# Hybrid DeltaNet, MoBA and RG-LRU block: norm weights and identity packed with the input into two transfers, first roundings and lows dealt in pairs, z's products waiting for each operand apart

## The reference, cut to what matters

```python
def rms_norm(x, w):
    xf = x.astype(jnp.float32)
    y = xf * lax.rsqrt(jnp.mean(xf * xf, axis=-1, keepdims=True) + NORM_EPS)
    return (y * w.astype(jnp.float32)).astype(x.dtype)

for l in range(DEPTH):
    h = rms_norm(x, norm_mix[l])
    proj = h @ w_in[l]
    (dq, dk, dv, dz, da, db, mq, mk, mv, lx, ly, gates) = split_columns(proj)
    y_dn = gated_deltanet(dq, dk, dv, dz, ...) @ dn_out[l]
    y_mb = moba_attention(mq, mk, mv) @ mb_out[l]
    y_lru = rg_lru_branch(lx, ly, ...) @ lru_out[l]
    ...
    x = x + mixed @ w_o[l]
    h = rms_norm(x, norm_ffn[l])
    gate, up = jnp.split(h @ ffn_in[l], 2, axis=-1)
    x = x + (jax.nn.silu(gate) * up) @ ffn_down[l]
return rms_norm(x, norm_final)
```

## Time and profile before

| | us |
|---|---|
| median of 3 runs | 909.99 |
| lowest and highest of them | 909.69, 910.98 |
| profiled execution: span, first to last instruction | 907.7 |
| TensorE busy in it | 895.2 |
| VectorE busy | 664.6 |
| ScalarE busy | 510.9 |

### The profile page before, as it was taken

How to read it: one execution, slowest core, us unless ns; L and a number is a source line. 1 busy time by engine, 2 the same in 40 slices (tenths; PEclk the granted TensorE clock), 3 DMA queues, 4 the chain that set the end, 5 groups by cost and what they waited for, 6 DMA issues and landing times.

```text
span 907.7 us, 13854 instructions
## 1 busy us (share of the span) xinstructions
PE 895.2 (99%) x5436; PEld 763.3 (84%) x5436; DVE 664.6 (73%) x1102; ACT 510.9 (56%) x871; POOL 2.4 (0%) x6
## 2 busy tenths in 40 slices
PE   8999999999999999999999999999999999999996
PEld 5999898888888888888779998988888888888885
DVE  6879877778958665756688798767988675665656
ACT  7586555685446444445475866558744554444443
POOL 0000000000000000000000000000000000000000
PEclk9999999999999999999999999999999999999999
DMA  8645436657665667677655343386567467768761
GB/s 308 196 159 163 145 113 160 232 201 241 211 209 159 216 210 247 201 226 250 204 166 182 123 164 124 109 233 231 195 205 241 149 216 217 246 191 259 223 203 47
DMA packets 111985, 176.37 MB, mean 194 GB/s; under 512 B 65584, under 2 KB 71472, under 8 KB 111920
## 3 DMA queue, kind: packets, MB, share of 16 engines
q1 hardware_dynamic: 111632, 175.40, 60.3%
q10 hardware_dynamic: 288, 0.08, 0.0%
HBM read 167.06 MB, written 8.39 MB: 193 GB/s over the span
## 4 chain that ended last, share of the span: by engine, by line
PE 91%; DVE 4%; ACT 2%; DMA 1%; issue 1%; SPq 0%; ACTq 0%; DVEq 0%
PE bank L456 7%; PE bank L455 7%; PE bank L454 7%; PE bank L552 7%; PE bank L554 7%; PE bank L553 7%; PE bank L357 5%; PE bank L358 5%; PE bank L359 5%; PE bank L629 5%; PE bank L396 5%; PE bank L397 5%; PE bank L398 5%; PE bank L386 2%; PE bank L384 2%; PE bank L385 2%
## 5 line engine op out<-in xcount | busy, mean ns | idle before, releaser
L882 ACT CAST whi<-raw 128x1024 fp32r<-128x1024 f32 x292 | 305.8, 1053 | 295.1 <-PE bank L456 90.0
L1218 DVE TENSOR_TENSOR wlo<-raw,whi 128x1024 fp32r<-128x1024 f32 x292 | 349.8, 1217 | 63.4 <-ACT whi L882 60.6
L357 PE MATMUL bank<-ahi,whi 128*128 128x256 f32 x448 | 129.6, 289 | 0.8 <-DVE tmp L1268 0.8
L358 PE MATMUL bank<-alo,whi 128*128 128x256 f32 x448 | 126.6, 283 | 0.0
L359 PE MATMUL bank<-ahi,wlo 128*128 128x256 f32 x448 | 126.6, 283 | 0.0
L552 PE MATMUL bank<-whi,ahi 128*128 128x512 f32 x288 | 114.8, 399 | 1.5 <-DVE alo L1282 0.8
L554 PE MATMUL bank<-whi,alo 128*128 128x512 f32 x288 | 112.3, 390 | 0.0
L553 PE MATMUL bank<-wlo,ahi 128*128 128x512 f32 x288 | 112.2, 390 | 0.0
L454 PE MATMUL bank<-whi,ahi 128*128 128x512 f32 x288 | 112.2, 390 | 0.0
L456 PE MATMUL bank<-whi,alo 128*128 128x512 f32 x288 | 112.1, 389 | 0.0
L455 PE MATMUL bank<-wlo,ahi 128*128 128x512 f32 x288 | 112.0, 389 | 0.0
(11 more groups left out here) (268 smaller groups left out, 1297.0 us busy)
## 6 DMA issues: line engine op xcount, KB each, us to landing
raw<-stream_dram SPq DMA_DIRECT2D x292, 512.0 KB, 4.6
turned_dram<-proj SPq DMA_DIRECT2D x144, 32.0 KB, 1.8
proj<-turned_dram SPq DMA_DIRECT2D x18, 256.0 KB, 4.8
proj<-gbias_dram SPq DMA_DIRECT2D x12, 256.0 KB, 4.4
probs_dram<-proj SPq DMA_DIRECT2D x8, 192.0 KB, 4.0
proj<-probs_dram SPq DMA_DIRECT2D x2, 768.0 KB, 5.9
par<-params_dram SPq DMA_DIRECT2D x2, 556.5 KB, 8.1
x<-x_dram SPq DMA_DIRECT2D x2, 512.0 KB, 5.2
```

The source lines that it names most:

```text
L357: pe.matmul(dst, whi_of(m)[:, wcol], hi, start=first, stop=False, skip_group_check=True)
L358: pe.matmul(dst, whi_of(m)[:, wcol], lo, start=False, stop=False, skip_group_check=True)
L882: act.copy(whi_of(m), raw_of(m)).then_inc(*AC.up(("hi", m), "w"))
L1218: dv.tensor_tensor(wlo_of(m), raw_of(m), whi_of(m), ALU.subtract).then_inc(*DV.up(("lo", m), "w"))
```

## The change

The norm weights (32 columns), the identity (128) and x (2 x 1024) become one tensor `head` in memory and on the chip. Its first transfer holds the norm weights, the identity and the first token tile; its second holds the second tile. The two transfers of ScalarE's queue are gone, with their semaphores; those who waited for them wait for the first half of `head`. In layer 0, ScalarE rounds two blocks of tile 0 before its second cast of weights instead of four, and the later roundings come in pairs by tile; VectorE's low parts of tile 0 are dealt likewise, two before it scales its half of tile 1 and two after the second weights' low part. TensorE's parts of z keep their order, but inside a part the six products are ordered high by high (both blocks), high by low, low by high, and each pair waits for its own operand: the weights' high part and the rounded blocks, then the weights' low part, then each block's low part. Buffers behind `x` move by 640 bytes a partition.

```diff
--- before.py
+++ after.py
@@ -72,6 +72,9 @@
 NCON = _at
 
 
+NHEAD = 2 * L * KT + P
+
+
 class Signal:
 
 
@@ -97,7 +100,7 @@
         return self.sem, self.n - back
 
 
-def build(nc, wstream, params, gbias, consts, norms, final, x_in, ident_in, ab_in, mixture, turned, probs, out, known):
+def build(nc, wstream, params, gbias, consts, final, head_in, ab_in, mixture, turned, probs, out, known):
     ctx = ExitStack()
     with ctx:
         def sb(name, shape, dt=F32):
@@ -109,16 +112,14 @@
         raw = sb("raw", [P, RING, HALF])
         whi = sb("whi", [P, RING, HALF], F32R)
         wlo = sb("wlo", [P, RING, HALF], F32R)
-        x = sb("x", [P, 2, D])
+        head = sb("head", [P, NHEAD + 2 * D])
         ahi = sb("ahi", [P, KT, T], F32R)
         alo = sb("alo", [P, KT, T], F32R)
         proj = sb("proj", [P, NT, T])
         bhi = sb("bhi", [P, 12, T], F32R)
         blo = sb("blo", [P, 12, T], F32R)
         con = sb("con", [P, NCON])
-        ident = sb("ident", [P, P])
         par = sb("par", [P, NPAR])
-        nrm = sb("nrm", [P, 2 * L * KT])
         tmp = sb("tmp", [P, 2, 2 * T])
         tmq = sb("tmq", [P, 2 * T])
         Tm = sb("Tm", [P, 8, SUB])
@@ -131,13 +132,15 @@
         small = sb("small", [P, 308])
         wab = sb("wab", [P, KT, 16], F32R)
         rab = sb("rab", [P, L, KT, 8])
+        nrm, ident = head[:, 0:2 * L * KT], head[:, 2 * L * KT:NHEAD]
+        x = head[:, NHEAD:NHEAD + 2 * D].rearrange("p (t d) -> p t d", t=2)
         bank = [ctx.enter_context(nc.psum_tensor(f"bank{i}", [P, 512], F32)) for i in range(8)]
 
         loaded_raw = [sem(f"loaded_raw{i}") for i in range(RING)]
         loaded_x = [sem(f"loaded_x{i}") for i in range(2)]
-        loaded_final, loaded_ident = sem("loaded_final"), sem("loaded_ident")
+        loaded_final = sem("loaded_final")
         loaded_gb = [sem(f"loaded_gb{i}") for i in range(2)]
-        loaded_con, loaded_nrm, loaded_par, loaded_ab = (sem(n) for n in ("loaded_con", "loaded_nrm", "loaded_par", "loaded_ab"))
+        loaded_con, loaded_par, loaded_ab = (sem(n) for n in ("loaded_con", "loaded_par", "loaded_ab"))
         stored = sem("stored")
         written_mix, loaded_mix = sem("written_mix"), sem("loaded_mix")
         written_hid, loaded_hid = sem("written_hid"), sem("loaded_hid")
@@ -289,9 +292,9 @@
                     sp.wait_ge(*DV.at("w", ("lo", m - RING)))
                 sp.dma_start(raw_of(m), wstream[m // 2, :, (m % 2) * HALF:(m % 2 + 1) * HALF]).then_inc(loaded_raw[m % RING], 16)
 
-            sp.dma_start(x[:, 0, :], x_in[:, 0, :]).then_inc(loaded_x[0], 16)
+            sp.dma_start(head[:, 0:NHEAD + D], head_in[:, 0:NHEAD + D]).then_inc(loaded_x[0], 16)
             load(0)
-            sp.dma_start(x[:, 1, :], x_in[:, 1, :]).then_inc(loaded_x[1], 16)
+            sp.dma_start(head[:, NHEAD + D:], head_in[:, NHEAD + D:]).then_inc(loaded_x[1], 16)
             load(1)
             sp.wait_ge(loaded_x[0], 16)
             load(2)
@@ -556,10 +559,23 @@
 
             def z_in_turns(l):
 
+                def part(q, t):
+                    m, tok, dst = l * NH + q, slice(t * P, (t + 1) * P), bank[4 + t][:, :]
+                    kts = ((2 * q, slice(0, 512)), (2 * q + 1, slice(512, 1024)))
+                    pe.wait_ge(*AC.at("w", ("hi", m)))
+                    pe.wait_ge(*AC.at(l, ("mix", "hi", t, q)))
+                    for kt, col in kts:
+                        pe.matmul(dst, ahi[:, kt, tok], whi_of(m)[:, col], start=kt == 0, stop=False, skip_group_check=True)
+                    wait_split(l, q)
+                    for kt, col in kts:
+                        pe.matmul(dst, ahi[:, kt, tok], wlo_of(m)[:, col], start=False, stop=False, skip_group_check=True)
+                    for kt, col in kts:
+                        pe.wait_ge(*DV.at(l, ("mix", "lo", t, kt)))
+                        ins = pe.matmul(dst, alo[:, kt, tok], whi_of(m)[:, col], start=False, stop=kt == KT - 1, skip_group_check=True)
+                    return ins
+
                 for q, t in ((0, 0), (1, 0), (0, 1), (1, 1), (2, 0), (2, 1), (3, 0), (3, 1)):
-                    if t == 0:
-                        wait_split(l, q)
-                    ins = token_half(l, q, q, t, bank[4 + t][:, :])
+                    ins = part(q, t)
                     if q == 3:
                         ins.then_inc(*PE.up(("z", t)))
                     elif t == 1:
@@ -795,7 +811,7 @@
             pe.wait_ge(*DV.at(0, "zeros"))
             for i in range(8):
                 exact(bank[7][:, :], tmp[:, 0, 0:P], tmp[:, 0, :])
-            pe.wait_ge(loaded_ident, 16)
+            pe.wait_ge(loaded_x[0], 16)
             for l in range(L):
                 PE.layer = l
                 if l == 0:
@@ -909,15 +925,17 @@
                 hi(0)
                 squares_of(1)
                 x_scaled(l, 0)
-                x_round(l, "mix", 0, 0, (0, 1, 2, 3))
+                x_round(l, "mix", 0, 0, (0, 1))
                 hi(1)
                 x_scaled(l, 1)
+                x_round(l, "mix", 0, 0, (2, 3))
                 x_round(l, "mix", 0, 1, (0, 1, 2, 3))
                 hi(2)
                 x_round(l, "mix", 0, 0, (4, 5))
-                x_round(l, "mix", 0, 1, (4, 5, 6, 7))
+                x_round(l, "mix", 0, 1, (4, 5))
                 hi(3)
                 x_round(l, "mix", 0, 0, (6, 7))
+                x_round(l, "mix", 0, 1, (6, 7))
 
             def mix_norm(l):
 
@@ -1174,8 +1192,6 @@
                     hi(first + 4)
                 hidhi(1)
 
-            act.dma_start(nrm[:, :], norms).then_inc(loaded_nrm, 16)
-            act.dma_start(ident[:, :], ident_in).then_inc(loaded_ident, 16)
             AC.layer = 0
             for l in range(L):
                 AC.layer = l
@@ -1327,9 +1343,10 @@
                 lo(0)
                 x_scaled(l, 0)
                 root(l, 1)
+                split(0, 0, 1)
                 x_scaled(l, 1)
-                split(0, 0, 1, 2, 3)
                 lo(1)
+                split(0, 2, 3)
                 split(1, 0, 1, 2, 3)
                 lo(2)
                 split(0, 4, 5)
@@ -1720,7 +1737,7 @@
             DV.layer = 0
             step(dv.memset(tmp[:, 0, :], 0.0), "zeros")
             step(dv.memset(inv[upper, :, 0:SUB], 0.0))
-            dv.wait_ge(loaded_nrm, 16)
+            dv.wait_ge(loaded_x[0], 16)
             mixw = nrm[:, :].rearrange("p (l s k) -> p l s k", l=L, s=2)[:, :, 0, :]
             step(dv.tensor_scalar(mixw, mixw, ROOT, None, ALU.mult), "norms")
             for l in range(L):
@@ -1852,10 +1869,10 @@
     final = np.broadcast_to(A(norm_final)[None, :], (P, D))
     ab = win[:, :, 2048:2056].reshape(L, KT, P, 8).transpose(2, 0, 1, 3)
     xs = A(x).reshape(2, P, D).transpose(1, 0, 2)
+    head = np.concatenate([norms, np.eye(P, dtype=np.float32), xs.reshape(P, 2 * D)], 1)
 
     arrays = {"stream_dram": stream, "params_dram": par, "gbias_dram": gbias, "consts_dram": _constants(),
-              "norms_dram": np.ascontiguousarray(norms), "final_dram": np.ascontiguousarray(final),
-              "x_dram": np.ascontiguousarray(xs), "ident_dram": np.eye(P, dtype=np.float32),
+              "final_dram": np.ascontiguousarray(final), "head_dram": np.ascontiguousarray(head),
               "ab_dram": np.ascontiguousarray(ab)}
     known = {}
     for _ in range(3):
```

## The result

The changed kernel is slower: 921.65 us (median of 4 runs, 921.40 to 922.35) against 910.38 for the kernel before (4 runs beside it), a ratio of 1.0133 with a 95% interval of 1.0121 to 1.0145. Forecast were 909.2 us and a range of 908.5 to 910.5. In the profiled executions the span went from 907.7 to 919.9 us, by 12.2.

What follows compares the result with a forecast made beforehand. TensorE was taken to bound the kernel, 91% of the 907.7 us span. Terms -0.51 (roundings), 0 (waits) and -0.3 (landings) made -0.8 us, span 906.9, plus 2.3 around it: 909.2 us, range 908.5 to 910.5.

Steps and rivals of the forecast that it cites:

- the test named at the end: Closing list of signs that would prove the forecast wrong, among them the distance of z's products rising over 0.23 us.
- The roundings in pairs: Layer 0's start: two roundings moved behind tile 1's scaling bring second cast, second turning and z's products forward, -0.51 us.
- The finer waits: TensorE's z: each operand waited for apart gains nothing itself, but protects 0.3 of the 0.51 us from being lost.
- The cost of 40 waits: TensorE in z: 40 waits where there were 20, taken as 0, with bounds of 0 and 2.8 us.
- The transfers: Kernel start: without q10's mixed packets x's second half lands earlier and the first turning comes forward, -0.3 us (bounds 0, -0.38).
- by the byte count alone: Alternative view of x's second half landing, with the same bytes ahead of it: the transfers' gain would be near 0.
- Rival 1: Kernel start: the larger first head transfer lands late, at 6.9 us; net +0.4 us, 910.4 us; chance 0.08.
- Rivals 2: TensorE's z: the 40 waits cost 0.07 us each, net +2.0 us, 912.0 us; chance 0.03.
- 3: Layer 0's z: moved roundings or lows late by half a microsecond, products stall at 14.0, no gain, 910.0 us; chance 0.12.
- Rival 4: Outside the span: one issuing queue fewer to set up and empty gives more gain, at most 906.9 us; chance 0.05.
- The 2.3 us: Around the profiled span: the median of 909.99 lies 2.3 us above the 907.7 us span, carried unchanged into the forecast.
- The floor that I set at 10.04: Kernel start: TensorE is busy with zeros to 10.04 us at least, so the first turning gains 0.38 us at most.

Runs made afterwards that it cites:

- experiment 1: Kernel before, with only identity and norm weights allocated behind x, so later buffers move by 640 bytes; old transfers, lists and waits: 923.40 against 909.61 us, ratio 1.0150.
- experiment 12: Changed kernel with head allocated behind con, no unused bytes, all operands at one address modulo 256: 908.11 against 909.79 us for the kernel before, ratio 0.9981.
- experiment 9: Kernel before with 128 unused bytes ahead of wlo and 128 behind it, so only wlo moved: 922.47 against 909.79 us, ratio 1.0139.
- experiments 8: Kernel before with 64 unused bytes behind x: 924.86 against 910.24 us, ratio 1.0167.
- 15: Kernel before with 128 unused bytes ahead of alo and behind it, so only alo moved: 915.15 against 909.80 us, ratio 1.0058.
- experiment 2: Changed kernel with 384 unused bytes a partition behind head, making the shift 1,024 bytes: 908.00 against 909.61 us for the kernel before, ratio 0.9981.
- experiment 10: Changed kernel with 384 unused bytes behind head but the old lists and old z; only the transfers are new: 909.28 against 909.79 us, ratio 0.9996.
- experiment 11: Kernel before with the changed lists and new order of z, but its own transfers and addresses: 907.70 against 909.79 us, ratio 0.9979.
- 14, lists only, old z: Kernel before with ScalarE's and VectorE's dealt lists but the old order and waits of z: 909.77 us, ratio 0.9999.
- 13: Kernel before with eight already satisfied waits added to TensorE's list in layer 0's z, nothing else: 908.96 against 909.80 us, ratio 0.9992.
- experiment 5: Kernel before with 256 unused bytes behind x: 910.62 against 910.24 us, ratio 1.0004.

## Why the prediction was wrong

**The step that failed** is one that the text does not have. Its first paragraph reads "because the diff touches nothing later" (than the first 25 us), and its sum has three terms, none for the buffers that move by 640 bytes. That shift is priced at nothing without a word. It costs 13.8 us alone (experiment 1): 2,832 products of 512 columns whose distance rose by 5 to 6 ns. Sum for the changed kernel: +13.8 and -1.7 (experiment 12) make +12.1, and +11.3 was measured (interval +11.0 to +13.2). None of the four rivals has this mechanism; the closest is the test named at the end, "if the distance of z's products rose over 0.23", which is what happened, everywhere.

Shown is that the relative place of TensorE's operands decides (0, 256, 512, 1,024 and 8,192 bytes are free, 64, 128 and 640 slow, which fits a period of 256), that a common shift is free, and that the slow distances lie on both sides of a product with a misplaced operand. What inside TensorE or its reads does this was not found: the third distance of experiment 9, and why 256-column products gain in experiments 8 and 15, stay open.

**The terms of the sum**, read from the aligned versions, where the loss does not cover them. "From first turning to z's end" is the start of the small product behind z less the start of the first turning.

| | first turning | z's end | between |
|---|---|---|---|
| before | 10.42 | 24.24 | 13.82 |
| 2, all, padded | 10.62 | 23.78 | 13.16 |
| 10, transfers only | 10.71 | 24.46 | 13.75 |
| 11, lists and z only | 11.02 | 24.17 | 13.15 |
| 12, all | 10.73 | 23.86 | 13.13 |
| 14, lists only, old z | 10.38 | 24.19 | 13.81 |

- *The roundings in pairs, -0.51 us*: right in mechanism, a little small. With the new z the stretch is 0.69 us shorter (0.66 by experiment 2, 0.67 by 11). Relative to the first turning, the second came 2.65 us behind it in experiment 12 (13.38), where 13.21 - 10.42 = 2.79 was forecast and 3.30 stood before.
- *The finer waits, 0, but "0.3 of the 0.51 us would be lost" without them*: undersized. Without them all of it is lost: 13.81 against 13.82. The second turning did come 0.27 us earlier (13.45 for 13.72), as the text had it, but TensorE then stopped for low parts, the last time before the product at 21.37, and z's end did not follow. The dealt lists alone are worth nothing; the new z with the old lists was not run.
- *The cost of 40 waits, 0 (bound +2.8)*: right. Experiments 2, 11 and 12 have them and are faster; in 13 eight satisfied ones more cost nothing that shows.
- *The transfers, -0.3 us*: wrong in sign. The mixing of q10 was not what made DMA slow: the rate at 5.0 to 5.5 us is 205 to 229 GB/s without it (changed kernel, 2, 10, 12), 206 to 261 with it (before, 11, 14). What the prediction called the view "by the byte count alone" was right: the second half has 80 KB more ahead of it and is used at 8.60 (8.62 in experiment 10, 8.52 in 2) in place of 8.33, and the first turning, where it waited for ScalarE, moved from 10.42 to 10.71 in experiment 10 and 10.62 in 2. (At the 10.73 of experiment 12 no wait stands; its zeros end at about that time.) The rule of the Trainium skill (DMA: Bandwidth & Descriptors, "Queues, rings and completion order"), that an engine takes turns between queues packet by packet, is not contradicted; the slowdown that I hung on it is.
- *Rival 1, a late head*: no. 592 KB landed in 3.7 us, as fast as the 512 KB of the earlier trace rows in 3.8.
- *Rivals 2 and 3*: no. In experiment 12 the 42 products behind the second turning take 9.63 us (14.23 to 23.86), where 9.73 stood before, and no wait stands among them.
- *Rival 4, a gain outside the span*: no. In every profiled execution whose own time is known, the rest around the span is 1.8 or 1.9 us, with ScalarE's two transfers (experiment 1: 923.89 - 922.1; experiment 5: 910.79 - 908.9) and without (after: 921.67 - 919.9; experiment 10: 909.28 - 907.5). The 2.3 us that the text ahead of the prediction puts there set a median against the span of another execution; some 0.5 of it is scatter between executions.
- *Not foreseen*: TensorE's zeros do not end at a fixed time. The sixteen took 8.76 us before, 9.61 after and 9.73 in experiment 11, and in those two they, not ScalarE, held the first turning (no wait stands at it). The granted clock was full in all of them, and what moves them was not found. The floor that I set at 10.04 moves by about a microsecond from version to version.

For the aligned version (experiment 12, span 905.9, by 1.8 us less than before) the ledger is: -0.69 (lists and waits), +0.31 (transfers, the first turning), and some -1.4 that is left for later stretches. Of these the wait at 447 us, 0.9 us in the profile before, is the one found; 0.5 us stay open. The medians differ by 1.7, interval 0.9 to 2.5. So where the start was to give 0.8 us it gave 0.4, and 1.4 of the 1.8 us by which the span is shorter came from stretches that the prediction did not look at.

## What to carry to other kernels

A new buffer, or a longer one, shifts all that is allocated behind it: keep the stationary operands (those that are loaded ahead, here `ahi`, `alo`, `bhi` and `blo` in the 512-column products) and the streaming ones (`whi`, `wlo`) of long runs of products at one address modulo 256 bytes, put odd-sized buffers behind them, and compare the mean ns of an untouched group of products before and after each edit. When a kernel is 91% one engine in its chain, ask of each edit what it does to the price of that engine's commonest instruction, not only to what stands ahead of it. An edit that brings an operand earlier may pay only if the consumer's waits are cut to the same grain, as the dealt lists did here.

## What the runs showed of the hardware

- A 128 x 512 product in float32r came every 227 ns with stationary and streaming operand at one address modulo 256 bytes, and every 232 to 234 with 64, 128 or 640 bytes between them: 1.3 to 1.7% of this kernel. 256-column products took 279 to 282 ns in place of 283 (the group of 448 with `alo` or `wlo`).
- The distances on both sides of a product with a misplaced operand are long: 396 and 397 ns recorded around `alo`, 390 for the third.
- DMA moved 205 to 229 GB/s from 5.0 to 5.5 us with one queue and 206 to 261 with two; from 7.5 to 8.0 it moved 377 to 451.
- One DMA issue of SyncE took 1.47 in place of 0.45 us where a packet of the queue named "instruction" fell beside it, and a wait of 0.9 us stood 16 us later; seen together, not proved.
